# A block of attention, HGRN2 and expert-choice experts followed by a conformer block: per-block hand-over in the experts, third norm in eight banks

## The reference, cut to what matters

```python
def expert_choice_ffn(h, w_router, w_gate, w_up, w_down):
    ...
    top_w, top_idx = lax.top_k(affinity.transpose(0, 2, 1), cap)      # 16 experts, cap = 64 of 512 tokens
    xe = jax.vmap(lambda hb, ib: hb[ib])(h, top_idx)
    hid = jax.nn.silu(jnp.einsum('becd,edf->becf', xe, w_gate)) * jnp.einsum('becd,edf->becf', xe, w_up)
    ye = jnp.einsum('becf,efd->becd', hid, w_down) * top_w[..., None].astype(h.dtype)
    combine = lambda yb, ib: jnp.zeros((S, D), h.dtype).at[ib.reshape(-1)].add(yb.reshape(-1, D))
    return jax.vmap(combine)(ye, top_idx)
...
x = x + gate2 * expert_choice_ffn(h, ...)          # end of the first block
...
xn = rmsnorm(h, g_mix[l])                           # start of the second: "the third norm" of the kernel
z = xn @ w_in[l] + b_in[l]
```

## Time and profile before

| | us |
|---|---|
| median of 3 runs | 2069.59 (2068.82 to 2070.51) |
| the profiled execution | 2067.35 |
| its span, first to last instruction | 2065.6 |
| TensorE busy | 1916.0, 93% of the span |
| VectorE (DVE) busy | 684.5, 33% |
| ScalarE (ACT) busy | 462.8, 22% |
| DMA | 513.42 MB, mean 249 GB/s |
| mean granted TensorE clock | 0.97 of full speed |

### The profile page before, as it was taken

How to read it: one execution, slowest core, us unless ns; L and a number is a source line. 1 busy time by engine, 2 the same in 40 slices (tenths; PEclk the granted TensorE clock), 3 DMA queues, 4 the chain that set the end, 5 groups by cost and what they waited for, 6 DMA issues and landing times.

```text
span 2065.6 us, 20340 instructions
## 1 busy us (share of the span) xinstructions
PE 1916.0 (93%) x8678; PEld 1151.8 (56%) x8678; DVE 684.5 (33%) x944; ACT 462.8 (22%) x685; POOL 32.7 (2%) x41
## 2 busy tenths in 40 slices
PE   6999979999789999998989999998899999999998
PEld 5876756567544344343434334343344478888887
DVE  6474465376421110212011011211039742322234
ACT  5347445313210000010100001010030432222223
POOL 0000000000000000000000000000040000000000
PEclk9999989999989999999999999999999999999999
DMA  8211110485679999999999999999960105322211
GB/s 302 87 49 49 62 36 27 159 295 219 278 300 414 421 421 421 421 421 421 421 421 422 420 421 421 422 421 421 384 212 29 41 31 163 102 92 92 102 62 41
DMA packets 131775, 513.42 MB, mean 249 GB/s; under 512 B 8035, under 2 KB 70627, under 8 KB 81379
## 3 DMA queue, kind: packets, MB, share of 16 engines
q1 hardware_dynamic: 127312, 487.95, 59.5%
q10 hardware_dynamic: 4374, 24.18, 3.1%
HBM read 510.00 MB, written 2.10 MB: 248 GB/s over the span
## 4 chain that ended last, share of the span: by engine, by line
PE 70%; DMA 18%; DVE 6%; ACT 3%; issue 2%; POOL 0%; SPq 0%; ACTq 0%; DVEq 0%; POOLq 0%
PE ps L1139 10%; PE ps L1100 9%; DMA work<-in_w_exp_up 9%; DMA ring<-in_w_exp_up 7%; PE ps L1304 5%; PE ps L540 5%; PE ps L1265 4%; PE ps L1264 4%; PE ps L1263 4%; PE ps L556 3%; PE ps L1028 3%; PE ps L558 3%; PE ps L557 3%; PE ps L739 2%; PE ps L1125 2%
## 5 line engine op out<-in xcount | busy, mean ns | idle before, releaser
L1100 PE MATMUL ps<-work 128*64 128x512 f32 x1208 | 326.1, 594 | 20.2 <-DMA work<-in_w_exp_up 20.2
L1100 PE MATMUL ps<-ring,work 128*64 128x512 f32 x712 | 216.7, 594 | 13.2 <-DMA ring<-in_w_exp_up 13.2
L1100 PEld LDWEIGHTS ps<-work 128*64 128x64 f32 x1208 | 109.5, 137 | 191.1 <-issue 150.7
L2233 DVE TENSOR_TENSOR work<-work,ps 64x512 f32<-64x512 f32 x64 | 42.0, 691 | 463.8 <-ACT work L1670 463.2
L1670 ACT ACTIVATE work<-ps 64x512 f32<-64x512 f32 x64 | 32.6, 584 | 723.9 <-PE ps L1100 723.9
L1139 PE MATMUL ps<-work 128*64 128x512 f32 x576 | 140.7, 641 | 5.2 <-issue 5.2
L540 PE MATMUL ps<-work,ring 128*128 128x512 f32 x320 | 138.9, 592 | 0.7 <-issue 0.7
L1263 PE MATMUL ps<-xh,wh 128*128 128x512 f32 x352 | 137.0, 389 | 0.0
L1265 PE MATMUL ps<-xh,wl 128*128 128x512 f32 x352 | 136.9, 389 | 0.0
L1264 PE MATMUL ps<-xl,wh 128*128 128x512 f32 x352 | 136.9, 389 | 0.0
L2366 DVE TENSOR_TENSOR wl<-ring,wh 128x2048 fp32r<-128x2048 f32 x33 | 75.6, 2292 | 180.2 <-ACT wh L1758 180.2
(11 more groups left out here) (343 smaller groups left out, 2596.9 us busy)
## 6 DMA issues: line engine op xcount, KB each, us to landing
work<-in_w_exp_gate SPq DMA_DIRECT2D x76, 1024.0 KB, 26.7
work<-in_w_exp_up SPq DMA_DIRECT2D x75, 1024.0 KB, 26.9
work<-in_w_exp_down SPq DMA_DIRECT2D x72, 1024.0 KB, 26.4
ring<-in_w_exp_up SPq DMA_DIRECT2D x45, 1024.0 KB, 27.0
ring<-in_w_exp_gate SPq DMA_DIRECT2D x44, 1024.0 KB, 26.5
ring<-in_w_exp_down SPq DMA_DIRECT2D x42, 1024.0 KB, 26.9
ring<-in_w_in SPq DMA_DIRECT2D x27, 1024.0 KB, 6.1
work<-in_ada_w ACTq DMA_DIRECT2D x16, 1024.0 KB, 6.0
```

The source lines that it names most:

```text
L1100: i = e.matmul(PS[64 * gu:64 * gu + 64, fb, :], at(XET + 128 * k + 64 * z, 64), flat(key)[:, 512 * fb:512 * fb + 512], start=(k == 0), sto ...
```

## The change

Six edits that belong together:

1. TensorE signals each of the four column blocks of the last k of an expert (four counts instead of two at k = 7, so 18 an expert; the gate and up piece of k = 7 are both released by the last). ScalarE's Silu of block fb waits for its own block.
2. The transposes of a block are a function, `turn_up`. Blocks 0 and 1 come ahead of the down product; the product starts when block 0 is copied; blocks 2 and 3 are transposed ahead of pieces 2 and 4 (last expert: ahead of pieces 1 and 2, whose pieces cover one block each).
3. In the last expert the routing weights are transposed ahead of k = 4 instead of behind gate/up, and ScalarE copies them ahead of the Silu.
4. The last expert's down pieces are 512 rows by 512 adjacent columns, one transfer each with runs of 2 KB; the halves of the result are columns 0 to 511 and 512 to 1023.
5. Behind the sum of the first half ScalarE takes one square root (of the first chunk's value; it is overwritten later).
6. The third norm's transposes use eight banks: blocks 0 to 5 with each chunk, blocks 6 and 7 behind the last. The dense products wait for bank u to be emptied of block u.

```diff
@@ last_reader
-            if kind == "eg":
-                return s["x_gu"], 16 * key[1] + 2 * key[2] + 1
-            if kind == "eu":
-                return s["x_gu"], 16 * key[1] + 2 * key[2] + 2
+            if kind in ("eg", "eu"):
+                return s["x_gu"], 18 * key[1] + (18 if key[2] == KD - 1 else 2 * key[2] + (1 if kind == "eg" else 2))
@@ SP
-                    r0, c0 = 512 * (key[2] % 4), 256 * (key[2] // 4)
-                    for dh in range(2):
-                        src = t["w_exp_down"][NE - 1, r0:r0 + 512, 512 * dh + c0:512 * dh + c0 + 256].rearrange("(k p) n -> p k n", p=128)
-                        e.dma_start(piece(key)[:, 4 * dh:4 * dh + 4, :], src).then_inc(ring[slot], 16)
+                    r0, c0 = 512 * (key[2] % 4), 512 * (key[2] // 4)
+                    src = t["w_exp_down"][NE - 1, r0:r0 + 512, c0:c0 + 512].rearrange("(k p) n -> p k n", p=128)
+                    e.dma_start(piece(key, 4), src).then_inc(ring[slot], 16)
@@ TensorE, last expert
-            def last_down():
-
-                e.wait_ge(s["x_hc"], 4 * NE)
+            def last_down(turn_up):
+
...
                     e.wait_ge(*got[key])
                     st = n // 4
+                    if n < 4:
+                        e.wait_ge(s["x_hc"], 4 * NE - 3 + n)
+                        if n in (1, 2):
+                            turn_up(n + 1)
@@ TensorE, every expert
+                    if (ex, k) == (NE - 1, 4):
+                        weights_back(p)
...
-                            if fb == 3:
+                            if (fb == 3 and k < KD - 1) or (k == KD - 1 and gu == 1):
                                 i.then_inc(s["x_gu"], 1)
...
                     if p + 1 < NE // 2:
                         gather(p + 1)
-                    weights_back(p)
-                for fb in range(4):
+                        weights_back(p)
+
+                def turn_up(fb):
                     e.wait_ge(s["x_hd"], 4 * ex + fb + 1)
...
+                turn_up(0)
+                turn_up(1)
                 if ex == NE - 1:
-                    last_down()
+                    last_down(turn_up)
                     break
                 for n in range(8):
                     key = ("ed", ex, n)
                     e.wait_ge(*got[key])
-                    if n == 0:
-                        e.wait_ge(s["x_hc"], 4 * ex + 4)
-                        if ex > 0:
-                            e.wait_ge(s["x_ym"], 2 * ex)
+                    if n % 2 == 0:
+                        e.wait_ge(s["x_hc"], 4 * ex + n // 2 + 1)
+                        if n in (2, 4):
+                            turn_up(1 + n // 2)
+                    if n == 0 and ex > 0:
+                        e.wait_ge(s["x_ym"], 2 * ex)
@@ TensorE, third norm
             def t3_free(k):
                 if k < 4:
                     e.wait_ge(s["x_hd"], 60 + k + 1)
+                elif k < 6:
+                    e.wait_ge(s["x_ym"], 24 + 2 * k)
                 else:
-                    e.wait_ge(*turned_k(3, k - 4))
+                    e.wait_ge(s["x_ca"], 57 + k)
...
-                for k in range(4):
+                for k in range(6):
...
-            for k in range(4, KD):
+            for k in (6, 7):
                 t3_free(k)
                 for c in range(TC):
-                    i = e.transpose(bank(k - 4, 128, 128 * c), at(XS3 + 1024 * c + 128 * k, 128), ident)
+                    i = e.transpose(bank(k, 128, 128 * c), at(XS3 + 1024 * c + 128 * k, 128), ident)
...
-                        e.wait_ge(*turned_k(3, 4 + u))
+                        e.wait_ge(*turned_k(3, u))
@@ ScalarE
+            def expert_weights_back(p):
+                e.wait_ge(s["x_ot"], p + 1)
+                e.activation(at(OHWT, 512), bank(7), ACT.Copy).then_inc(s["x_oc"], 1)
...
-                e.wait_ge(s["x_gu"], 16 * ex + 16)
+                if ex == NE - 1:
+                    expert_weights_back(p)
                 for fb in range(4):
+                    e.wait_ge(s["x_gu"], 18 * ex + 15 + fb)
                     e.activation(rows(64, 128, SG + 512 * fb, 512), PS[0:64, fb, :], ACT.Silu).then_inc(s["x_sl"], 1)
...
             own(e.activation(at(st3a, 4), at(st3, 4), ACT.Identity, bias=vec("eps6")))
+            own(e.activation(at(st3 + 4, 1), at(st3a, 1), ACT.Sqrt))
...
-            turned(3, [0, 1, 2, 3], lambda k, src: e.activation(xn(k), src, ACT.Copy, scale=vcol("gmix", k)), lambda: None)
+            turned(3, range(KD), lambda k, src: e.activation(xn(k), src, ACT.Copy, scale=vcol("gmix", k)), lambda: None)
```

More of the change, by code:

```diff
@@ L1063, in combine_half @@
                         e.wait_ge(s["x_ca"], 55 + m)
-                    e.matmul(bank(6 + m % 2), at(OHWT + 128 * tc, 128), raw(YE + 256 * st, [(512, 2), (1, 256)]), start=True, stop=True).then_inc(s["x_cb"], 1)
-            def last_down():
-                e.wait_ge(s["x_hc"], 4 * NE)
+                    e.matmul(bank(6 + m % 2), at(OHWT + 128 * tc, 128), at(YE + 512 * st, 512), start=True, stop=True).then_inc(s["x_cb"], 1)
+            def last_down(turn_up):
                 e.wait_ge(s["x_ym"], 2 * NE - 2)
@@ L1074, in last_down @@
                     st = n // 4
+                    if n < 4:
+                        e.wait_ge(s["x_hc"], 4 * NE - 3 + n)
+                        if n in (1, 2):
+                            turn_up(n + 1)
                     for k in range(4):
                         for dh in range(2):
-                            i = e.matmul(PS[64 * dh:64 * dh + 64, 4 + st, 0:256], at(HIDT + 64 * (4 * (n % 4) + k), 64), piece(key)[:, 4 * dh + k, :],
+                            i = e.matmul(PS[64 * dh:64 * dh + 64, 4 + st, 0:256], at(HIDT + 64 * (4 * (n % 4) + k), 64), piece(key, 4)[:, k, 256 * dh:256 * dh + 256],
                                          start=(n % 4 + k == 0), stop=(n % 4 + k == 6))
@@ L1673, in _ @@
                         gather(p + 1)
-                    e.wait_ge(s["x_ot"], p + 1)
-                    e.activation(at(OHWT, 512), bank(7), ACT.Copy).then_inc(s["x_oc"], 1)
+                        expert_weights_back(p)
                 for fb in range(4):
@@ L1678, in _ @@
                     e.activation(at(HIDT + 256 * fb, 256), bank(6 + fb % 2, 256), ACT.Copy).then_inc(s["x_hc"], 1)
[L1681 removed]
+            half_x = lambda c, st: at(X + 1024 * c + 512 * st, 512)
             for c in range(TC):
                 e.wait_ge(s["x_ca"], 57 + c)
[L1684 removed]
+                own(e.activation(at(XNT + 512 * (c % 2), 512), half_x(c, 0), ACT.Square, scale=1.0 / 32, accum_out=at(st3 + c, 1)))
             own(e.activation(at(st3a, 4), at(st3, 4), ACT.Identity, bias=vec("eps6")))
+            own(e.activation(at(st3 + 4, 1), at(st3a, 1), ACT.Sqrt))
             for c in range(TC):
                 e.wait_ge(s["x_ca"], 61 + c)
[L1689 removed]
+                own(e.activation(at(XNT + 1024 + 512 * (c % 2), 512), half_x(c, 1), ACT.Square, scale=1.0 / 32, accum_out=at(st3b + c, 1)))
                 e.activation(at(st3 + 4 + c, 1), at(st3b + c, 1), ACT.Sqrt, bias=at(st3a + c, 1)).then_inc(s["r_a"], 1)
[L1691 removed]
+            turned(3, range(KD), lambda k, src: e.activation(xn(k), src, ACT.Copy, scale=vcol("gmix", k)), lambda: None)
             def o2_hi(i):
@@ L2254, in add_half @@
                 m = 4 * st + tc
-                xa = raw(X + 1024 * tc + 256 * st, [(512, 2), (1, 256)])
+                xa = at(X + 1024 * tc + 512 * st, 512)
                 e.wait_ge(s["x_cb"], 57 + m)
@@ L2258, in add_half @@
                     e.wait_ge(s["x_ca"], 56)
-                e.tensor_tensor(xa, xa, bank(6 + m % 2).rearrange("p (a n) -> p a n", a=2), ALU.add).then_inc(s["x_ca"], 1)
+                e.tensor_tensor(xa, xa, bank(6 + m % 2), ALU.add).then_inc(s["x_ca"], 1)
             for st in range(2):
```

9 lines of the change are left out of this document (3 added, 6 removed).

## The result

The changed kernel takes 2058.52 us (median of 4 runs, 2057.82 to 2060.39) where the kernel before took 2069.28 (four runs) beside it: ratio 0.995, 95% interval 0.9937 to 0.9964. It is faster by 0.5%, beyond the 0.2% that can be told apart, and by more than forecast: 2063.0 was predicted and the range ended at 2060.0. The profiled execution is one of the four, 2058.82 us with a span of 2057.0.

What follows compares the result with a forecast made beforehand. The weight stream at 421 GB/s was taken to bound the experts, TensorE close behind. Gains of 0.8 + 3.4 + 1.3 + 1.1 = 6.6 us gave 2063.0 us from the median 2069.59; range 2060.0 to 2067.0.

Steps and rivals of the forecast that it cites:

- Part 1: First experts: earlier down product closes the weight stream's hole at 630 to 640 us; 0.8 us, bounds 0 and 1.2.
- Part 2: Last up weight to end of last down product: earlier product start and full clock; 3.4 us, bounds 1.8 and 4.5.
- Part 3: Third norm: early square root takes the 1.28 us table load out of the chain; 1.3 us, bounds 0 and 1.3.
- Part 4: Third norm's last scaling to first dense matmul: eight banks, fewer transposes behind it; 1.1 us, bounds 0 and 2.2.
- the 60 that was named as a sign: Experts: TensorE's waits for up weights should grow to 60 us or more; staying at 35 would prove the forecast wrong.
- as one: Behind 1525.29 us: 45.06 us of dense matmuls without transfers follow, so everything there should move together.
- A: Last expert: last down weights set the end, or the clock stays low; gain 4.1 to 5.2 us, chance 0.21.
- B: Experts: TensorE's win is real time in every expert, 15 x 2.5 us, about 2028 us; chance 0.02.
- C: Experts: low clock in the waits becomes a bound, kernel slower, 2102 us with 20 us per expert; chance 0.03.
- D: Third norm: load stays or eight banks' copies take the time; total gain 4.5 us, 2065.1 us; chance 0.08.
- E: Behind 1525 us: something is late anyway and little gain reaches the end; 2067 to 2069 us; chance 0.07.
- F: Last expert: changes between transposes and product cost over 0.09 us, taking 1.9 us from the gain; 2064.9 us; chance 0.05.

Runs made afterwards that it cites:

- e7: Changed kernel with the old hand-over (Silu behind all gate/up, four transpose groups ahead of the product) in experts 0 to 14; 2058.47 us against 2067.52 before.
- e10: Changed kernel with the last expert transposing and copying all four blocks ahead of its down product; 2059.45 us against 2068.36 for the kernel before.
- e1: Changed kernel without its early small square root; 2059.90 us against 2068.01 for the kernel before (0.9965).
- e6: Kernel before plus matmuls of constants, read by nothing, in TensorE's waits around the third norm; 2066.23 us against 2067.52 (0.9993).
- e11: Changed kernel with four banks at the third norm plus two unread transposes in each of the first three chunks; 2060.26 us against 2068.36 before.
- e9: Kernel before with only the eight banks for the third norm's transposes added; 2064.37 us against 2068.36 (0.998).
- e2: Changed kernel with the third norm's transposes back in four banks; 2063.66 us against 2068.01 for the kernel before (0.998).
- e3: Changed kernel with the hand-over and early routing-weight transposes undone in all experts; 2063.64 us against 2068.01 for the kernel before (0.9979).
- e8: Changed kernel plus matmuls of constants, read by nothing, around the fourth norm; 2057.75 us against 2067.52 for the kernel before (0.9955).
- e4: Changed kernel with each last-expert down piece fetched as two transfers in 1 KB runs; 2060.37 us against 2068.01 for the kernel before (0.9966).

## Why the prediction was wrong

The four places are right, and parts 1 to 3 came within 0.3 us of their sizes. Part 4 failed: it took the low clock at the norm as given. The sum was short by 4.5 us of the median, and the range by 1.5. From profile to profile it is 2060.75 against 2058.82, 1.9 us, which is the 1.9 of part 4; the 1.2 of the fourth norm cancels against the later start of the experts (0.9) and the 0.3 of part 3.

**Part 1** (0.8): right, column A is 1.0. e7 shows that fifteen experts together give it, and starts of single matmuls show where. With the old order (e7 against the changed kernel) k = 7 of expert 4 starts 5.4 us later after the first gate/up matmul, k = 7 of expert 5 only 0.98, and from there to the last expert it stays at 0.8 to 1.0. So the first experts do gain time, since they are not yet at the pace of the weights (in the changed kernel 47 to 56 us from the start of one to the next, and about 60 from the sixth on). In expert 5 TensorE catches up with the stream, and of the gain only the hole's one microsecond is left. Expert 0 and the next four are not separated by a run; that the hole comes from expert 0 is read from where it lies. The waits for up weights grew to 52 us, not to the 60 that was named as a sign.

**Part 2** (3.4): right, 3.47. The product started 4.82 us behind k = 7 (4.86 expected); the fifth piece was waited for 0.48 us (0.5 expected); the clock was 1.00 as assumed. A group of transposes inside the product costs less than the 0.66 taken: the pieces behind one start 2.27 us after the piece before (1486.76, 1489.03, 1491.30), the next without one starts 1.78 later (1493.08 in the trace), so 0.49. The 1.6 us counted for the clock come out too: before, the first and the fifth piece started 8.6 us apart, where four pieces at 1.73 to 1.78 take 7.0. e10 shows what the split was good for: without it 1.1 us are lost, mostly to the clock. The Trainium skill's rule ("TensorEngine Tiling (Array Packing)", Key Properties) that a change of tiling mode drains the engine would need room inside these 0.49 us, which also hold the four transposes; no row shows an idle gap there, so the trace doesn't bear it out as a cost here.

**Part 3** (1.3): 1.01, shown by e1. The load left the chain whole; 0.27 us came back as a later start of the next square. The Trainium skill's drain of 1.38 us with each load ("ScalarE: Activation LUTs") isn't in these traces: taking the load out and putting it back moved the chain by 1.01 us, less than the load itself.

**Part 4** (1.1): this is the step that failed; it measured 3.02. The prediction read the low clock of the earlier trace rows as a fixture that the change leaves where it is: "if it comes back at the same distance from the last scaling". It counted 14 transposes at 0.215 us and 0.65 us of slow dense work. In the changed kernel the clock never fell there: 14 transposes in 1.74 us (0.87 + 0.87 of the chain) instead of 3.01, dense work at full speed from the first matmul: 1.27 + 0.65 = 1.92 us, the whole miss of the part. Its upper bound, 2.2 with the clock full, was too low as well and has no working: 14 transposes at full speed give 4.8 - 1.8 = 3.0. Of the 3.02 us won, 1.63 are clock and 1.39 banks (e6, e11), where the prediction had 1.7 for the banks and nothing for the clock.
What kept the clock up is several edits at once. One profile each shows it: old hand-over, load in the chain, four transposes a chunk (before): 0.51 over 5 us. Old hand-over, load, six (e9): 0.66. New, no load, four (e2): 0.76 and 0.90. New, load, six (e1) and old, no load, six (e3): 1.00, D = 1.64. So six transposes with either of the others were enough in these executions. Each profile is a single draw of the clock, and e2's times lie above what its profile shows; that more than one edit has a part in it fits all of them, a rule for how is not shown. What the clock's share costs is the better shown: filling the waits and nothing else removed it twice (e6 against the kernel before, e11 against e2).

**The fourth norm** (not in the sum): the prediction moved everything behind 1525 "as one". Columns E and G did, to 0.1 us, but F did not: 6.88 in the profile before, 5.46 to 6.17 in the twelve others. F goes with the clock: in 1680 to 1700 us it was 0.83 in the kernel before, 0.91 in the changed one and in e6, and 1.00 in e2, e8 and e9, the three with 5.46 to 5.47. Two of the kernels in that band have no edit of the last expert at all (e6, e9), which speaks for chance; but the kernel before has one profile, and whether 6.88 is usual for it isn't shown. It is 1.16 of the 8.56 us between the two profiles.

**The base.** The forecast was hung on 2069.59, a median of three. Fifty runs of the kernel before later gave medians of 2067.5 to 2068.4. With 2068.0 under it the same sum gives 2061.4, and the changed kernel's 2058.5 to 2059.0 is then 2.4 to 2.9 us away, of which part 4 is 1.9. The first measured gain of 10.8 us holds 0.9 to 1.8 us of this chance; the range allowed 0.9 for it. The bounds were also added up wrongly: with part 1 at its own upper bound of 1.2 they give 9.2 us and 2060.4, not 8.8 and 2060.8; less the 0.9 that is 2059.5, still above the measured time.

**Rivals.** A (its 2.3 for part 2 should be 2.1 by its own landing time, and its 5.2 doesn't follow from its terms; e4 measured 2.2): the last down weights do bind, by 0.5 us, and would bind by 1.5 with runs of 1 KB (e4); the clock came back. B (its 2028 is the span less 37.5 us; from the median and with the other parts it would be 2026) and C: out, from the sixth expert on the pace is the stream's with the old order and the new, and TensorE waits more at a clock that fell less often (mean 0.984 for 0.970). D: out, e1 and e9 show both edits at work. E: out, columns E and G carry everything through. F: out, a group costs 0.49 with its transposes.

## What to carry to other kernels

- A low granted clock beside a chain is part of the chain's length, and a change that shortens or fills the waits ahead of it can remove it. Price such a stretch at both clocks and let the upper bound be the full one: here 20 transposes and their bank waits were 4.66 us at the low clock and 3.03 at the full one.
- Where all of a long stage runs at the pace of one stream, look only at its holes and behind its last piece. Fifteen quicker experts gave 1.0 us; the last one gave 3.5. A lead that TensorE wins ahead of the stream (5.4 us by the fifth expert) is lost again.
- Cut the span at events and compare the pieces: all but two repeated within 0.3 us, where medians of five runs couldn't tell 1 us, and they showed that 2.5 us of the first 10.8 lie outside the four parts. Keep the times beside them: one profile of e2 doesn't account for its median.

## What the runs showed that was not expected

- Matmuls that nothing reads, in waits, made a kernel's chain shorter by 1.63 us (e6) without touching its work; two idle transposes a chunk took 1.04 us off the column of e2 (e11).
- The clock at a norm follows more than the wait directly ahead: with the load's 1.28 us back in the chain it stayed at 1.00 (e1), with two transposes fewer a chunk it fell (e2).
- The first square behind ScalarE's idle time starts 0.36 us after its input in the changed kernel, 0.09 us after it without the early root (e1). The cause is open.
- The part of the kernel that no edit touches, ahead of the first gate/up matmul, took 583.6 to 587.5 us in thirteen profiles. Of all the columns it varies most between kernels that have the same code there; the cause is open.
